# One wide product and one wide addition on GpSimd in place of six and eight narrow ones, where it rotates a projected tile

## The reference

```
h = x + 1/2 * SwiGLU_1(RMSNorm(x))                     # d_ff 2816
u = RMSNorm(h);  proj = u @ w_in                       # qa ka va qb kb vb
rope on qa, ka, qb, kb: [x1*cos - x2*sin, x2*cos + x1*sin]
group A: sliding-window attention, 8 q heads, 2 kv heads, sinks
group B: differential attention, 4 heads with two maps each
h = h + concat(out_a, out_b) @ w_out
h = h + 1/2 * SwiGLU_2(RMSNorm(h));  y = RMSNorm(h)
```

## Time and profile before

| what | before |
|---|---|
| median of 3 runs | 1029.38 us |
| the profiled execution | 1029.78 us, its span 1027.9 us |
| TensorE busy | 1010.7 us, 98% of the span |
| VectorE busy | 802.5 us, 78% |
| ScalarE busy | 566.8 us, 55% |
| GpSimd busy | 160.0 us, 16% (289 instructions) |
| granted TensorE clock | 0.998 of full speed over the span |

### The profile page before, as it was taken

The page is one execution under the profiler, slowest core; times in us unless marked ns, Lnnn a source line. Parts: engine busy times, 40 slices in busy tenths (PEclk is TensorE's granted clock), DMA queues, the critical chain, the costliest instruction groups (busy, mean ns, idle before and its releaser), DMA issues.

```text
span 1027.9 us, 19437 instructions
## 1 busy us (share of the span) xinstructions
PE 1010.7 (98%) x7572; PEld 985.7 (96%) x7572; DVE 802.5 (78%) x1229; ACT 566.8 (55%) x984; POOL 160.0 (16%) x289
## 2 busy tenths in 40 slices
PE   9999999999999999999999999999999999999996
PEld 9999999999999999987888899999999999999996
DVE  6998777888678895478767768698877788778886
ACT  7635644666456663345435556435654665555655
POOL 0000000000010035233545205000100010010001
PEclk9999999999999999999999999999999999999999
DMA  6335666665665546230121212416566666657542
GB/s 248 94 102 160 180 154 176 174 158 151 180 177 147 138 122 212 64 98 22 53 70 55 98 42 82 116 61 183 155 152 163 186 151 168 176 155 179 140 109 93
DMA packets 37578, 137.33 MB, mean 134 GB/s; under 512 B 5424, under 2 KB 6576, under 8 KB 37360
## 3 DMA queue, kind: packets, MB, share of 16 engines
q1 hardware_dynamic: 29424, 107.52, 30.2%
q0 software_dynamic: 8064, 28.58, 17.4%
HBM read 131.10 MB, written 4.98 MB: 132 GB/s over the span
## 4 chain that ended last, share of the span: by engine, by line
PE 56%; DVE 3%; POOL 1%; ACT 1%; issue 1%; DVEq 0%; ACTq 0%; POOLq 0%
PE acc L990 29%; PE acc L888 17%; PE acc L1137 3%; PE acc L1175 1%; PE acc L1003 1%; PE acc L1245 1%; PE acc L1165 1%; POOL side L2588 1%; PE acc L1131 0%; POOL q_b L2566 0%; PE acc L1204 0%; PE acc L1208 0%; PE acc L1179 0%; DVE probs L2392 0%; DVE side L2289 0%
## 5 line engine op out<-in xcount | busy, mean ns | idle before, releaser
L1884 DVE TENSOR_TENSOR w_lo<-raw,w_hi 128x1024 fp32r<-128x1024 f32 (+4 forms) x187 | 196.5, 1053 | 109.8 <-ACT w_hi L1351 94.1
L990 PE MATMUL acc<-c_hi,w_lo 128*128 128x288 f32 x952 | 282.0, 296 | 0.0
L990 PE MATMUL acc<-c_hi,w_hi 128*128 128x288 f32 x952 | 280.9, 295 | 0.0
L990 PE MATMUL acc<-c_lo,w_hi 128*128 128x288 f32 x952 | 277.6, 292 | 0.0
L1351 ACT ACTIVATE w_hi<-raw 128x1024 fp32r<-128x1024 f32 (+4 forms) x157 | 140.8, 897 | 86.4 <-PE acc L990 56.8
L1519 ACT ACTIVATE comb<-acc 128x288 f32<-128x288 f32 x224 | 92.0, 411 | 165.6 <-PE acc L990 163.5
L990 PEld LDWEIGHTS acc<-c_lo,w_hi 128*128 128x128 f32 x952 | 180.8, 190 | 0.0
L990 PEld LDWEIGHTS acc<-c_hi,w_hi 128*128 128x128 f32 x952 | 179.0, 188 | 0.0
L990 PEld LDWEIGHTS acc<-c_hi,w_lo 128*128 128x128 f32 x952 | 178.6, 188 | 0.0
L990 PE MATMUL acc<-h_hi,w_hi 128*128 128x288 f32 x574 | 170.7, 297 | 3.3 <-ACT comb L1519 1.7
L990 PE MATMUL acc<-h_hi,w_lo 128*128 128x288 f32 x574 | 169.8, 296 | 0.0
(11 more groups left out here) (264 smaller groups left out, 1805.9 us busy)
## 6 DMA issues: line engine op xcount, KB each, us to landing
raw<-in_w1st SPq DMA_DIRECT2D x17, 768.0 KB, 4.3
raw<-in_w2st SPq DMA_DIRECT2D x17, 768.0 KB, 4.2
raw<-in_w_qk SPq DMA_DIRECT2D x13, 512.0 KB, 3.9
raw<-in_w1sd SPq DMA_DIRECT2D x8, 768.0 KB, 4.3
raw<-in_w2sd SPq DMA_DIRECT2D x8, 768.0 KB, 4.3
raw<-in_w1gu SPq DMA_DIRECT2D x10, 512.0 KB, 4.3
raw<-in_w2gu SPq DMA_DIRECT2D x10, 512.0 KB, 3.8
raw<-in_w1st SPq DMA_DIRECT2D x9, 512.0 KB, 5.2
```

The costliest lines, as they stand in the source:

```text
L990: m = nc.tensor.matmul(acc[:, banks[side_of(p)], 0:HALF], w_part[:, col:col + P], x_part, start=n in (P1, P5, P2) and k == 0 and e == 0, s ...
L1884: return nc.vector.tensor_tensor(cols, src, hi.bitcast(FP32), ALU.subtract).then_inc(split_ready, 1)
```

## The change

`rotated` adds the 512 prompt columns in one instruction instead of eight of 64 columns, and the product with the sines is one instruction of 576 columns instead of six of 96. The waits stay: the addition still waits until the product is done.

```diff
             def rotated(dst):
 
-                for part in range(8):
-                    cols = slice(part * SEQ // 8, (part + 1) * SEQ // 8)
-                    m = nc.gpsimd.tensor_tensor(dst[:, cols], rope_x[:, cols], turned[:, cols], ALU.add)
-                return m
+                return nc.gpsimd.tensor_tensor(dst[:, 0:SEQ], rope_x[:, 0:SEQ], turned[:, 0:SEQ], ALU.add)
...
                 gp.wait_ge(turn_done, b + 1)
-                for part in range(6):
-                    cols = slice(part * TOK // 6, (part + 1) * TOK // 6)
-                    steps[0] += 1
-                    nc.gpsimd.tensor_tensor(turned[:, cols], turned[:, cols], trig[:, 1, cols],
-                                            ALU.mult).then_inc(gp_step, 1)
-                gp.wait_ge(gp_step, steps[0])
+                then(nc.gpsimd.tensor_tensor(turned[:], turned[:], trig[:, 1, :], ALU.mult))
                 gp.wait_ge(x_out, b + 1)
```

## The result

| what | before, same chip | after |
|---|---|---|
| median | 1029.50 us (6 runs, 1029.35 to 1029.67) | 1033.25 us (6 runs, 1031.87 to 1034.69) |
| profiled execution | 1029.78 us, span 1027.9 | 1033.12 us, span 1031.1 |
| VectorE busy | 802.5 us | 812.8 us |
| GpSimd busy | 160.0 us | 130.4 us |
| granted TensorE clock, mean | 0.998 | 0.996 |

The ratio is 1.0029 [1.0019, 1.0039]: 0.29%, or 3.0 us slower; the two medians lie 3.75 us apart. The forecast of 1030.9 us is 2.35 us too low. 1033.25 us is 0.05 us above the top of the range as it was written (1033.2), and above the 1029.8 to 1032.4 of the forecast itself. The prediction gave 0.57 to a change of less than 0.2%; the interval of the ratio reaches from just under that mark to well above it. GpSimd was relieved of 30 us, and VectorE, whose queue is the same, is busy 10 us longer, 7.6 us of it between 400 and 610 us.

What follows compares the result with a forecast made beforehand. TensorE, 98% busy, was taken to bound the kernel. The terms -0.85 - 0.2 + 1.0 + 0.9 + 0.2 + 0.1 + 0.3 + 0.1 made +1.5 us on 1029.4: 1030.9 us, range 1028.6 to 1033.2 us.

Steps and rivals of the forecast that it cites:

- qa3: Tile qa3: L2387 and L2397 are held by the wide product and addition, making TensorE late by +1.0 us.
- kb0: Tile kb0: the same holds, partly absorbed by VectorE's 0.40 us wait for scores; TensorE late by +0.9 us.
- qb0: Tile qb0: the first scaled pair of probabilities comes about 1.2 us later, costing TensorE +0.2 us.
- qa1: Tile qa1: costs TensorE +0.1 us; the remaining 1.1 us on VectorE dies in its 1.91 us wait.
- 0.4 us won back: Behind tile qa3: VectorE regains 0.1 us in two small sums and 0.3 us in short waits before copies and fills.
- The wait for `q_diag`: Tile qb0, before the scores L1179: TensorE's one wait on GpSimd goes, -0.85 us.
- qb1: Tile qb1: L2402 and the addition come within 0.05 us of each other; between 0 and +0.7 us, taken +0.3.
- qb3: Tile qb3: the wide instructions cost TensorE +0.1 us.
- qa2: Tile qa2: VectorE reaches L2291 0.25 us earlier, bringing TensorE -0.2 us with the step before.
- The first (VectorE slips in): Rival: VectorE gets in between product and addition, so qa3 costs +0.5 and kb0 +0.15 us; 1029.0 us, chance 0.22.
- The second (holds pass through at nearly every tile, 1033.7 us): Rival: VectorE's delays behind L2291 reach TensorE at nine tiles; +4.3 us, 1033.7 us, chance 0.20.
- The third: Rival: half of TensorE's 4.5 us idle time between 440 and 610 us goes; 1027.1 us, chance 0.08.

Runs made afterwards that it cites:

- e3: The whole change at tiles qa3, kb0 and qb1 only, the other ten narrow as in the kernel before; 1033.94 us, ratio 1.0029 to before.
- e4: The whole change except at tiles qa1, qa3, kb0, qb1 and qb3, which stay narrow as before; 1030.09 us, ratio 0.9990 to before.
- e1: Kernel before with only the product made one piece of 576 columns, additions still eight of 64; 1030.38 us, ratio 0.9997.
- e6: Kernel before, GpSimd unchanged, with VectorE doing five awaited 64-column fills of an unused tile behind L2291 at qa3 and kb0; 1030.87 us, ratio 1.0006.
- e7: Kernel before with product and addition cut to one column each, the other columns' rotation left out; 1029.56 us, ratio 0.9998.
- e5: Kernel before with the product as two pieces of 288 columns and the addition as two of 256, at all tiles; 1029.93 us, ratio 0.9999.
- e8: The repeat: the change run again unaltered, beside runs of the kernel before on the same chip; 1033.25 us, ratio 1.0032.
- e9: Kernel before with GpSimd's rotation at qa3 and kb0 replaced by zero fills of the same columns, twice each; one run, 1029.83 us.
- e12: e5's form plus e11's twelve extra unread TensorE matmuls near the end of the second feed-forward network; 1031.21 us, ratio 1.0006 to before.
- e2: Kernel before with only the addition made one piece of 512 columns, products still six of 96; 1029.99 us, ratio 0.9991.
- e10: Kernel before with the product as two pieces of 288 columns and the addition in one piece of 512; one run, 1031.63 us.
- e11: Kernel before plus twelve unread TensorE matmuls in the second feed-forward network, meant to fill a wait that stayed unfilled; 1032.61 us, ratio 1.0013.

## Why the prediction was right in its mechanism and short in size

**What a wide instruction costs, and what lies beside it.** The durations: 1.42 and 1.28 to 1.29 us, predicted 1.43 and 1.29. L2387 and L2397 at 1.03 and 1.23 us, predicted about 1.1 and 1.2. VectorE did not slip in between product and addition. qa3, kb0, qb0 and qa1 came out within 0.06 us of their terms, and e3 and e4 show that they are where they should be. One sign was off: TensorE's wait before L1197 behind kb0 is 0.95 us and not 1.4, since 0.42 us of the delay comes earlier, at L1240. The prediction's 0.38 us for L2397 alone was the shortest of four executions that all lie beside GpSimd's instructions; undisturbed it takes 0.32 (e1, e6, e7). The terms do not hang on it.

The step from VectorE to TensorE can now be told as a number. This is how long after GpSimd's start at qa3 L2397 ends, by the rows above and the earlier trace rows:

| kernel | L2397's end after the product's start | against before | TensorE's shift |
|---|---|---|---|
| e7 | 1.11 | -0.44 | 0 |
| before | 1.55 | | |
| e5 | 1.68 | +0.13 | 0 |
| e1 | 1.99 | +0.44 | +0.20 |
| e6 | 2.36 | +0.81 | +0.49 |
| after, e3 | 2.90 | +1.35 | +1.02 |

VectorE has 0.24 to 0.33 us of slack there, and beyond it TensorE is late one for one. Wide product, fills, and both wide instructions give one line, and being early gives nothing. The prediction had 0.4 us won back. This is also what stands against traffic: e5 reads and writes as much as the change at -0.91 us, and e6 leaves GpSimd's work as it was at +0.92.

**The wait for `q_diag`.** Predicted -0.85; -1.11 in every kernel that loses it. The matmuls behind it start 1.01 us earlier and the group is 0.10 us shorter (1.24 to 1.14). The 0.85 is an idle time between the modelled end of a pipelined matmul and the next start. The shift of the starts is the measure, and I hadn't it.

**The step that failed: "between 0 and +0.7, taken +0.3" at qb1.** The tie went to GpSimd, in the change, its repeat and e3 alike: L2402 took 1.59 us in place of 0.51, and it costs +0.80. Between the two ends of a tie there is no middle; +0.3 was a value that neither outcome gives. It is the largest part of the 0.8 us by which the middle stage's sum was short: 0.5 here, 0.2 each at qb3 and qa2, less 0.26 at `q_diag`.

**qb3**, predicted +0.1, cost 0.32. The addition starts at 566.05 us, and this sum of one column comes 0.07 us behind it:

```profile
566.12 1.25 DVE L2405 TENSOR_TENSOR st<-st,lam 128x1 f32<-128x1 f32 x1
```

Before it took 0.24 us. Some of the 1.0 us goes into a wait of VectorE's ahead of its first L2476. The second comes 0.3 us later against TensorE than it did, and L888 stands 0.43 us for it. **qa2**, predicted -0.2, brought 0: VectorE gets to L2291 sooner, but the step that waits for it starts no sooner.

**The clock.** No term for it stood in the sum. Single runs of before, with the mean clock of each:

| mean granted clock | before beside e1 to e4 | before beside e5 to e8 | before beside e9 to e12 | the change |
|---|---|---|---|---|
| 0.998 | 1029.74 (10 runs) | 1029.75 (10) | 1029.47 (9) | 1032.20, 1031.87; repeat 1032.78 |
| 0.997 | 1030.16 (3) | 1029.67 (8) | 1029.34 (2) | 1033.57; repeat 1032.13 |
| 0.996 | 1031.09 (11) | 1031.30 (4) | 1031.46 (7) | 1033.12, 1034.69; repeat 1033.32 (5) |
| 0.995 | | | | 1033.38 |
| 0.994 | 1032.08 (6) | 1032.35 (4) | 1032.08 (4) | |

In the profiles a mean of 0.998 goes with no slow stretch ahead of the last few microseconds, and 0.996 with one. So the kernel before falls as well, in some executions and not in others, and the medians of its runs with and without lie 1.4 to 2.0 us apart. At equal clock the change costs 2.3 us (1032.03 against 1029.74) and, in the repeat, 2.0 us (1033.32 against 1031.30, five runs and four) and 3.0 (one run, 1032.78 against 1029.75); the shift of 2.3 and the 0.28 us at the end make 2.6. Of the 3.75 us between the first two medians some 1.2 to 1.4 are therefore left for the clock: all six runs of before there lie under 1029.7 us, the level without the fall. Whether the change makes the fall more likely is open: before had a mean of 0.996 or less in 36 of 82 runs, the change in 8 of 13. e1, e2, e4 and e5, which are no slower than before, have it in 30 of 44 runs (last section), so being slow is not what brings it. But all of these have wider instructions on GpSimd, and e6, where GpSimd's are as before, has it in 3 of 10 runs beside before's 8 of 29; against it, e7, which has hardly any, has it in 6 of 10. That wide instructions raise the chance is not excluded, and no run was made to test it.

**The rivals.** The first (VectorE slips in) falls by L2397's 1.23 us. The second (holds pass through at nearly every tile, 1033.7 us) is nearer to the measured time than the forecast is, but by luck: of its nine tiles at 0.6 us each, kb1, qb2 and kb2 gave 0 and qa1, qb0 and qb3 0.15 to 0.32, and the clock gave the rest. The third falls, and e7 bounds it: without any rotation to speak of only 1.06 us are to be had, not half of 4.5.

**The best form.** e2, e4 and e5 are 0.9 us ahead of the kernel before in the trace, and by ratio 0.9991 [0.9982, 1.0000], 0.9990 [0.9981, 0.9999] and 0.9999 [0.9990, 1.0007]: about 0.1% at best. The gain of 0.9 us in the trace is nearly all of the 1.1 us that e7 leaves; in the medians e5's is not told from nothing.

## What to carry to other kernels

The instructions of a helper engine that holds up a busy one should be cut by the other's slack, not by its own overhead: two pieces of some 0.75 us in place of one of 1.42 changed +2.3 us into -0.9, by the traces. Don't add up the costs of two holds that follow each other; walk through them in order of time, since the first decides whether the second hits. And where two instructions arrive within the precision of a record, price both outcomes and take one of them.

## What the runs showed of the hardware

A few hundredths of a microsecond decide a stop of more than 0.8: at qb1 L2402 is recorded 0.03 us ahead of the addition and takes 1.59 us in place of 0.51. GpSimd starts its next instruction 0.07 us after its last. VectorE came 0.25 us after the product at qa3, and lost 0.91 us by it (1.23 for 0.32).

A fill on GpSimd does not stop a VectorE sum with two inputs in SBUF (0.15 us under it, and 0.15 undisturbed in e7), while a GpSimd instruction that reads does (1.03 us). A scaling with one input is stopped by both (0.52 and 1.23 us, 0.32 alone). The Trainium skill, SBUF — State Buffer, "Who interferes with whom", says that two inputs contend with GpSimd's reads and not with its mere writes, and counts the scaling among the operations that can take both ports; the four numbers agree.

TensorE's granted clock fell to 1.2 GHz for 3.4 us near the end, about a wait of 1.8 us in the change (1.8 to 2.9 us in e3, e4, e6, e7, e10 and e11), and did not in before, e1, e2, e5, e9, e12 and the repeat, whose waits there are 1.7 to 2.0 us. In e6 it fell while TensorE still waited. In e7 and e10 it fell at 397 us as well, where TensorE's waits in the 3 us ahead are 0.2 us, with ten matmuls of one column behind the last of them: a wait of 1.8 us is not needed either. One fall costs 1.3 us net in the change's profile, and 1.4 to 2.0 us between medians of before. It comes in any version of this kernel: e1, e2, e4 and e5 have a mean clock of 0.996 or less in 8, 7, 8 and 7 of 11 runs. What decides it, the runs do not show.
